# Two-block transformer on one core: attention heads laid into neighbouring weight chunks, and three small moves

## What is computed

```python
for l in range(DEPTH):                       # DEPTH = 2, N_A = 1
    if l == N_A:                             # keys, values, forget gate, once
        kvf = rmsnorm(x, kv_norm) @ w_kvf
        f_logit = (kvf[..., 2 * FOX_WIDTH:] + b_f)
        c_sh = jnp.cumsum(jax.nn.log_sigmoid(f_logit), axis=1)
    x = x + 0.5 * swiglu(rmsnorm(x, ffn_norm[l, 0]), ...)
    h = rmsnorm(x, mix_norm[l])
    mk, mv = split(mem_n @ mem_w_kv[l])      # 4 memory heads of 128
    if l < N_A:
        gate_b, gate_c, u, qm = split(h @ a_w_in)
        y_tok = gate_b * causal_depthwise_conv(gate_c * u, a_conv_w)
        y_mem = memory_attention(qm, mk, mv)
        x = x + concat([y_tok, y_mem]) @ a_w_out
    else:
        q, qm = split(h @ b_w_q)             # 8 heads of 128, 4 memory heads
        y_tok = forgetting_attention(q, k_sh, v_sh, c_sh)
        y_mem = memory_attention(qm, mk, mv)
        x = x + concat([y_tok, y_mem]) @ b_w_out
    x = x + 0.5 * swiglu(rmsnorm(x, ffn_norm[l, 1]), ...)
```

## Time and profile before

| | |
|---|---|
| median of 3 runs | 1873.25 us (1873.0 to 1874.36) |
| the profiled execution: its time, its span | 1875.29 us, 1873.5 us |
| TensorE busy | 1819.4 us, 97% of the span, 9737 matmuls |
| VectorE, ScalarE, GpSimd busy | 65%, 50%, 16% |
| granted TensorE clock, mean | 0.993 of full |
| read from HBM | 318.24 MB, 170 GB/s |

### The profile page before, as it was taken

The page is one execution under the profiler, slowest core; times in us unless marked ns, Lnnn a source line. Parts: engine busy times, 40 slices in busy tenths (PEclk is TensorE's granted clock), DMA queues, the critical chain, the costliest instruction groups (busy, mean ns, idle before and its releaser), DMA issues.

```text
span 1873.5 us, 27530 instructions
## 1 busy us (share of the span) xinstructions
PE 1819.4 (97%) x9737; PEld 1539.3 (82%) x9737; DVE 1211.2 (65%) x1523; ACT 936.3 (50%) x1394; POOL 299.1 (16%) x255
## 2 busy tenths in 40 slices
PE   8899999999999999999999989999999999999998
PEld 6678888888877888888888878888888888778886
DVE  5866755767775665576746756674667656656664
ACT  4455545434456544464545445554554455555553
POOL 1011021211201001210022930002005021020012
PEclk9999999999999999999999999999999999999999
DMA  6326555555521665555555535555555555345553
GB/s 218 130 74 197 180 201 180 180 180 180 180 91 53 195 191 185 195 180 187 193 184 182 186 123 180 193 187 190 182 191 174 185 189 174 108 146 180 188 193 134
DMA packets 215000, 320.29 MB, mean 171 GB/s; under 512 B 6024, under 2 KB 167056, under 8 KB 214672
## 3 DMA queue, kind: packets, MB, share of 16 engines
q1 hardware_dynamic: 213616, 313.45, 50.3%
q0 software_dynamic: 1024, 5.64, 0.8%
q10 hardware_dynamic: 288, 0.23, 0.0%
HBM read 318.24 MB, written 1.06 MB: 170 GB/s over the span
## 4 chain that ended last, share of the span: by engine, by line
PE 91%; DVE 4%; ACT 3%; issue 1%; DMA 1%; DVEq 0%; POOL 0%; POOLq 0%; ACTq 0%; SPq 0%
PE PS L656 26%; PE PS L661 13%; PE PS L663 13%; PE PS L662 13%; PE PS L654 13%; PE PS L650 4%; PE PS L651 2%; PE PS L768 2%; DVE W_lo L1275 2%; PE PS L803 1%; PE PS L786 1%; PE PS L730 1%; ACT U L1096 1%; ACT U L1086 1%; PE PS L919 1%
## 5 line engine op out<-in xcount | busy, mean ns | idle before, releaser
L1275 DVE TENSOR_TENSOR W_lo<-W_raw,W_hi 128x1024 fp32r<-128x1024 f32 x598 | 775.5, 1336 | 292.7 <-ACT W_hi L1012 270.8
L656 PE MATMUL PS<-XN,W_hi 128*128 128x512 f32 x2072 | 740.1, 396 | 0.0
L1012 ACT ACTIVATE W_hi<-W_raw 128x1024 fp32r<-128x1024 f32 x598 | 598.6, 1050 | 176.4 <-PE PS L663 114.5
L654 PE MATMUL PS<-XN,W_lo 128*128 128x256 f32 x2072 | 579.2, 280 | 2.7 <-DVE W_lo L1275 2.7
L656 PEld LDWEIGHTS PS<-XN,W_hi 128*128 128x128 f32 x2072 | 389.6, 188 | 80.2
L654 PEld LDWEIGHTS PS<-XN,W_lo 128*128 128x128 f32 x2072 | 391.4, 189 | 16.6 <-DVE W_lo L1275 3.0
L1809 POOL TENSOR_TENSOR SX<-U,SX 128x512 fp32r<-128x512 f32 (+1 forms) x98 | 128.5, 1315 | 1141.5 <-ACT SX L1079 1141.5
L661 PE MATMUL PS<-W_hi,SX 128*128 128x512 f32 x780 | 303.9, 390 | 1.1 <-DVE W_lo L1275 1.1
L662 PE MATMUL PS<-W_lo,SX 128*128 128x512 f32 x780 | 303.0, 389 | 0.0
L663 PE MATMUL PS<-W_hi,SX 128*128 128x512 f32 x780 | 303.0, 389 | 0.0
L1025 ACT ACTIVATE T<-PS 128x512 f32<-128x512 f32 x152 | 91.0, 599 | 410.5 <-PE PS L656 410.3
(11 more groups left out here) (166 smaller groups left out, 1532.1 us busy)
## 6 DMA issues: line engine op xcount, KB each, us to landing
W_raw<-in_ffn_w_gate_up SPq DMA_DIRECT2D x88, 1024.0 KB, 5.0
W_raw<-in_mlp_w SPq DMA_DIRECT2D x64, 1024.0 KB, 5.2
W_raw<-in_ffn_w_down SPq DMA_DIRECT2D x44, 1024.0 KB, 4.8
W_raw<-in_od_w_in SPq DMA_DIRECT2D x36, 1024.0 KB, 5.1
W_raw<-in_a_w_in SPq DMA_DIRECT2D x14, 1024.0 KB, 4.9
W_raw<-in_mem_w_kv SPq DMA_DIRECT2D x8, 1024.0 KB, 5.1
W_raw<-in_w_kvf SPq DMA_DIRECT2D x8, 1024.0 KB, 5.4
W_raw<-in_ev_w_in SPq DMA_DIRECT2D x6, 1024.0 KB, 6.3
```

Of the source, the lines that this page charges most:

```text
L654: mm(bank[:, S:], wT(W_lo, slot, k, fb), xn[:, k, 0, :], start=False, stop=False)
L656: last = mm(bank, wT(W_hi, slot, k, fb), both, start=False, stop=k == KD - 1)
L1012: A(W_hi[:, slot, halves(h)], W_raw[:, slot, halves(h)], ACT.Copy).then_inc(w_hi, 1)
L1275: V.tensor_tensor(W_lo[:, slot, halves(h)], W_raw[:, slot, halves(h)], W_hi[:, slot, halves(h)], ALU.subtract).then_inc(w_lo, 1)
```

## The change

In `make_plan` the order of the stages changes and the attention stages are marked as woven: a head's steps now stand inside chunks of the neighbouring stages. `steps` says which step stands in which chunk. Step s does `values` of head s-3, `transposes` of head s-2 and `scores` of head s on TensorE; `output` of s-3, `normalise` of s-1 and `soft` of s on VectorE; `keep_pt` of s-2 and `exps` of s on ScalarE. `mem_q` goes ahead of `conv` and of `fox_q`, and `b_out` takes the rows of the memory heads first. Three small moves come with it: at the start the second load waits for the first, the tables wait for the fourth load instead of the second, and two of five dummies go while three new ones stand behind the turn of x; in the gated MLP the logarithm stands one pair of chunks later.

In the diff, the pieces are in this order: the plan, the loads on SyncE, an up and a down chunk on TensorE, a woven step on TensorE, the dummies and the turn of the gate's sums on TensorE, the staging and the gated MLP on ScalarE, a woven step on VectorE, the tables on GpSimd.

```diff
         if l == 0:
-            p.add("conv", "conv", 12, 12, w=w["a_w_in"])
             up("mem_q", w["a_w_in"], 3072, 2, post="copy", dest="mem_q0")
-            p.add("attend", "memory0", what=[("mem0", h) for h in range(4)])
+            p.add("conv", "conv", 12, 12, w=w["a_w_in"], steps={c: [c] for c in range(7)})
+            p.add("attend", "memory0", what=[("mem0", h) for h in range(4)], woven=True)
             down("a_out", w["a_w_out"], 1536)
         else:
-            up("fox_q", w["b_w_q"], 0, 4, post="copy", dest="fox_q")
             up("mem_q", w["b_w_q"], 1024, 2, post="copy", dest="mem_q1")
-            p.add("attend", "fox",
-                  what=[e for h in range(4) for e in (("fox", 2 * h), ("fox", 2 * h + 1), ("mem1", h))])
-            down("b_out", w["b_w_out"], 1536)
+            up("fox_q", w["b_w_q"], 0, 4, post="copy", dest="fox_q",
+               steps={c: [2 * c, 2 * c + 1] for c in range(4)})
+            p.add("attend", "fox", what=[("mem1", h) for h in range(4)] + [("fox", h) for h in range(8)],
+                  woven=True)
+            down("b_out", w["b_w_out"], 1536, order=[4, 5, 0, 1, 2, 3],
+                 steps={0: [8, 9], 1: [10, 11], 2: [12, 13], 3: [14]})
...
             def load(g, slot, src, ks, n):
                 if not isinstance(g, int) or g >= 2:
                     sp.wait_ge(w_lo, 2 * (g - 1))
+                elif g == 1:
+                    sp.wait_ge(raw_full[0], 16)
...
                  for fb, k in sorted(steps, key=lambda x: x[1]) if by_k else steps:
...
+                    if k == 3 and fb < len(woven):
+                        woven[fb]()
...
                 for t in range(TT):
-                    if first and t == 1 and st["src"] == "h" and not st["each"]:
+                    if first and st.get("weave"):
+                        if t == 0:
+                            pe.wait_ge(acc_read, st["u"])
+                    elif first and t == 1 and st["src"] == "h" and not st["each"]:
                         pe.wait_ge(h_done, st["h0"])
...
+                        if at == 2 and t < len(woven):
+                            woven[t]()
...
+            def woven_step(st, s):
+                if s == 0:
+                    pe.wait_ge(r_kept, st["n_rows"])
+                out, turned, scored = (woven_head(st, s - back) for back in (3, 2, 0))
+                if out is not None:
+                    values(heads[out]["unit"])
+                if turned is not None:
+                    transposes(turned)
+                if scored is not None:
+                    pe.wait_ge(acc_read, heads[scored]["q_use"])
+                    scores(heads[scored]["unit"])
...
-            for _ in range(5):
-                mm(PS[:, 0, :], T[:, 0:P], T[:, 0:512], start=True, stop=True)
+            idle_work(3)
...
                         turn(st)
+                        if g0 == 0:
+                            idle_work(3)
...
-                            if st.get("sums") and starts(i, s - 1):
+                            if s == 1 and sums_in(st, i):
                                 between, at = turn_sums, (1, 0)
...
+                elif st["name"] == "a_out" and j < 4:
+                    act.wait_ge(conv_done, j + 1)
+                elif st["name"] == "b_out":
+                    act.wait_ge(h_done, st["h0"] - before_heads(st) + 2 * j + 2)
...
                             if not (st["led"] and starts(i, s)):
                                 ahead(g0 + 2 * i + s, slots[s])
+                            if s == 0 and sums_in(st, i):
+                                act.wait_ge(f_v, 1)
+                                A(f_abs, f_abs, ACT.Exp, scale=-1.0).then_inc(f_a, 1)
+                                act.wait_ge(f_a, 2)
+                                A(f_abs, f_abs, ACT.Ln, bias=1.0).then_inc(f_a, 1)
+                                A(ST[:, 60:61], G[:, 0:1], ACT.Silu)
...
                             cross(g0 + 2 * i + s, u0 + 2 * i + s, pairs[s])
...
+            def woven_step(st, s):
+                out, scaled, scored = (woven_head(st, s - back) for back in (3, 1, 0))
+                if out is not None:
+                    output(heads[out]["unit"])
+                if scaled is not None:
+                    normalise(scaled)
+                if scored is not None:
+                    soft(scored)
...
-            pool.wait_ge(raw_full[1], 16)
+            pool.wait_ge(raw_full[1], 32)
             pool.dma_start(region(R["na_bias"], NA_H * SLOTS * GRID), a["na_bias"]).then_inc(bias_in, 16)
```

More of the change, by code:

```diff
@@ L500, in build_program @@
                 n_staged += st["n"]
-                before = stages[n - 1]
+                before = stages[n - 2 if stages[n - 1].get("woven") else n - 1]
                 before["next_down"] = st
                 st["each"] = before["kind"] == "glu" or before.get("dest") == "h"
-            if st["kind"] == "attend":
+                st["bank"] = [4, 6]
+            if st["kind"] == "attend" and not st["woven"]:
                 stages[n - 1]["next_attend"] = st
-        before_heads = lambda st: len(stages[stages.index(st) - 1]["what"])
+            if st["kind"] == "attend" and st["woven"]:
+                for near in (stages[n - 1], stages[n + 1]):
+                    if near.get("steps"):
+                        near["weave"] = st
+                if stages[n + 1].get("steps"):
+                    pair = stages[n + 1]["u"] % 2
+                    stages[n + 1]["low_banks"] = [2 * pair, 2 - 2 * pair]
+        before_heads = lambda st: len(stages[stages.index(st) - 1]["what"])
+        for n, st in enumerate(stages):
+            if st.get("low_banks"):
+                st["bank"] = st["low_banks"]
+            if st["kind"] == "norm":
+                st["down_bank"] = stages[n - 1].get("bank", [4])[0] if n else 4
+            if st["kind"] == "attend" and st["woven"]:
+                use = {q["name"]: q["u"] for q in stages[:n] if q["name"] in ("mem_q", "fox_q")}
+                for what, h in st["what"]:
+                    e = next(e for e in heads if e["st"] is st and (e["bias"] == "fox", e["h"]) == (what == "fox", h))
+                    e["q_use"] = use["fox_q" if what == "fox" else "mem_q"] + h // 2 + 1
         def e_out_done(n):
@@ L512, in e_out_done, with woven_head, row_block @@
                     return st["h0"] + n - st["a0"] + 1
+        def woven_head(st, s):
+            at = st["weave"]
+            return at["a0"] + s if 0 <= s < len(at["what"]) else None
+        def row_block(st, j):
+            return st["order"][j] if st.get("order") else j
         def raw_count(g, slot):
@@ L534, in build_program, with after_first, sums_in @@
         starts = lambda i, s=0: isinstance(i, int) and i == 0 and s == 0
-        def after_first(engine, n, body):
-            body(0)
-            repeat(engine, n - 1, lambda i: body(i + 1))
+        def after_first(engine, n, body, first=1):
+            for i in range(first):
+                body(i)
+            repeat(engine, n - first, lambda i: body(i + first))
+        def sums_in(st, i):
+            return bool(st.get("sums")) and isinstance(i, int) and i == 1
         block = ctx.enter_context(nc.Block())
@@ L888, in body @@
                                      first=s == 0 and (starts(i) or not st["raised"]),
-                                     between=between, at=at, by_k=st["led"] and starts(i, s))
+                                     between=between, at=at, by_k=st["led"] and starts(i, s),
+                                     woven=woven_steps(st, 2 * i + s) if "weave" in st else ())
                     if n > 1:
-                        after_first(pe, n // 2, body)
+                        after_first(pe, n // 2, body, 2 if st.get("sums") else 1)
                     if n % 2:
@@ L981, in _ @@
                         turn_heads(R["mla_kn"], 2 * pairs[b] - 2 * b, range(4 * b, 4 * b + 4))
-                elif kind == "attend":
-                    a0, m = st["a0"], len(st["what"])
+                elif kind == "attend" and not st["woven"]:
                     pe.wait_ge(acc_read, u0)
                     us = st["units"]
-                    if not st["paired"]:
-                        for u in us[opened(st):3]:
-                            scores(u)
                     for u in us:
@@ L997, in _ @@
                             scores(u + 2)
-                        if not st["paired"] and u + 3 in us:
-                            scores(u + 3)
                         values(u)
@@ L1166, in _ @@
                     else:
-                        repeat(act, loops, body)
-                    if early:
+                        repeat(act, loops, body, straight="weave" in st)
+                    if early and st["name"] != "fox_q":
                         stage_early(early)
@@ L1240, in _ @@
                     stage_early(st["next_down"])
-                elif kind == "attend":
-                    a0, m = st["a0"], len(st["what"])
```

(4 more changed lines are left out.)

145 lines of the change are left out of this document (85 added, 60 removed).

## The result

The changed kernel took 1877.87 us (median of 8 runs, 1874.61 to 1879.13), the kernel before 1873.12 us (8 runs, 1871.45 to 1874.78): a ratio of 1.0022, 95% interval 1.0013 to 1.0031. Forecast were 1873.5 us, within 1866.5 to 1880.5, with "same" likelier (0.52) than "slower" (0.27). The time lies in the range. The change is slower by 0.22% (0.13 to 0.31), just over the 0.2% that was put as the bound of what can be told; by the medians it is 4.75 us. And 1877.87 lies 0.9 us above the narrower range, 1870 to 1877, that stood for the forecast's own sum.

A forecast was written before the change was run, and what follows sets the result against it. TensorE was taken to bound the dense stage, so changes count only through its waits and low clock. Terms +11.6 - 7.5 - 1.6 - 2.4 = +0.1 us gave 1873.5 us, range 1866.5 to 1880.5.

The forecast's parts named there:

- Place 1: memory0, conv into a_out: stall 17.1, low clock 2.5, woven waits 0.3, less 8.3 removed: +11.6 us.
- The stall: Ahead of a_out: TensorE stands still until GpSimd's last conv chain and first low part are done, 17.1 us.
- The chain: GpSimd's operations for the last conv column block, then a_out's first low part: 14.5 us, starting 2.6 us after the last chunk.
- The clock: Behind the gap ahead of a_out: TensorE at the lower clock, 1.7 to 3.5 us lost, taken as 2.5.
- Place 2: fox, heads woven into fox_q and b_out: 12.4 us of losses removed; gap 2.4, clock 1.2, waits 1.3 added: -7.5 us.
- the rival in which VectorE's queue paces the woven chunks: Woven attention chunks: heads keep their earlier waits, fox_q chunks take over 9.8 us; 5 us more, 1878.5 us; 18%.
- Place 3: The gate in the gated MLP: 4.5 us of losses removed, waits of 1.4 and 1.5 added: -1.6 us.
- The second wait: At the gate: VectorE's split held by GpSimd's later bias tables, put at 1.5 of 0 to 4 us.
- Place 4: The start: earlier first matmul and third load, but norm factor behind the tables: -2.4 us, between -4.5 and +1.
- two rivals (1878.5 and 1879): VectorE's queue pacing woven chunks, 1878.5 us, 18%; a longer a_out stall, longer low clock and bad start, 1879 us, 12%.
- the seam is dearer: Into a_out: stall 19.0 us and low clock for 7 us, +2.9, plus the start's bad end, +3: 1879 us; 12%.

The follow-up runs named there:

- the filled stall: Changed kernel plus 80 dummy matmuls on TensorE between the last conv chunk and a_out: 1873.61 us, ratio 0.9996 to the kernel before.
- the first experiment: Changed kernel with GpSimd making a_out's first two low parts ahead of the last conv column block's chain: 1870.78 us, ratio 0.9980 to the kernel before.
- the kernel with the tables spread: Changed kernel with the gate's bias tables made piece by piece behind low parts of ffn_down on GpSimd: 1879.01 us, ratio 1.0030 to the kernel before.

## Why the prediction was right, and where it was not

**Place 1** was forecast at +11.6 us and measured at +12.2. The stall: 17.1 forecast, 17.65 measured. The chain from its first operation to the end of the first low part took 14.4 us where the prediction summed 14.5, which also decides between its two bounds for the stall (17.1 if the chain is faster without VectorE beside it, 19.0 if GpSimd is simply that slow). It began 3.2 us after the last chunk, not 2.6, since `by_rows` took 1.61 us, not 0.69, beside GpSimd's product of the block before. The clock: 2.5 forecast, 6.1 us at half measured, 3.1 lost; the filled stall shows that the standing still was its cause. With VectorE's split beside it the same pair of scalings took 3.88 us instead of 1.82 (in the first experiment, at 1100.62). The waits in the woven chunks, put at 0.3, did not occur here; three other executions have one, of 0.83, 0.43 and 0.34 us, for `normalise` in a woven `conv` chunk at 1047.

**Place 2** was forecast at -7.5 and measured at -7.7: a gap of 2.30 us (2.4), 1.7 us of clock (1.2, between 0 and 1.7), 0.3 us of waits in the woven chunks (1.3). The wait of `values` came in the third chunk of `b_out`, where the prediction had it, with 0.3 instead of 1 us. A `fox_q` chunk with its heads took 8.5 us (34.05 by four), where over 9.8 would have spoken for the rival in which VectorE's queue paces the woven chunks. So that rival is wrong: a head whose partners had a chunk's time waits for almost nothing. That -7.7 comes so close to -7.5 is in part luck: the waits were put 1.0 us too high and the clock 0.5 too low.

**Place 3** failed in size: -1.6 forecast, +0.6 measured. The two waits were 1.04 and 1.93 us, together 2.97 where 2.9 was put. What the sum lacks is the step behind them: 3.4 us at the low clock after the second gap, 1.7 lost, and half a microsecond at its edges. The prediction gives the clock a term at both seams and none here, and states no reason; the gap of 2.73 us before had no fall behind it. A gap of this size is followed by a fall in some executions and not in others (below), so each such gap should have had half a term. The second wait, put at 1.5 of 0 to 4 us, rests on a guess of the phase: that it came at 1.93 is luck.

**Place 4** was right in its mechanism: the first matmul of weights at 11.05 (11.2), the factor ready at 25.6 (25.9), the chunk at 30.66 (30.9). The forecast of -2.4 agrees with what was left in the pair of profiles at the next stage, 2.17 us, where TensorE waited for a split, longer than before. Timelines of TensorE, before and changed:

```profile
46.89 0.47 PE L661 MATMUL PS<-W_hi,SX 128*128 128x512 f32 x1 [1.09 <-DVE W_lo L1275]
44.72 0.47 PE L703 MATMUL PS<-W_hi,SX 128*128 128x512 f32 x1 [1.70 <-DVE W_lo L1373]
```

It agrees too with the 2 us over all profiled executions. In this pair 1.2 of it is left at the second turn of x, since the low clock at the end of the first attention lasted 6.82 us in the changed kernel, and in the kernel before half as long:

```profile
112.26:115.67 3.41, 2.98 (x14) 1.82 (x10) 0.43 (x1) 1.41 (x3) 2.50 (x2) 0.50 0.00 0
```

So the forecast of +0.1 missed the +3.9 of the last turn by 3.8, 2.2 of it at place 3, 1.2 at place 4, 0.6 at place 1, with place 2 the other way by 0.2. By its number the result is nearer to two rivals (1878.5 and 1879) than to the sum, and neither took place: the woven chunks hardly waited, and the chain took 14.4 us, not the 16.4 that a stall of 19.0 needs; of "the seam is dearer" only the longer low clock came, worth 0.6 us. That no change was forecast and a small one measured is thus a matter of place 3's missing term and of one late draw at the start. "The saving at the attention is paid back by the conv chain" is what happened, and the payback was for the most part avoidable (16.6 of 20.7 us): with the order of GpSimd's queue mended, the same weave, the repairs at the gate and `b_out` and the norm's factor ahead of the tables are together worth 1.3%.

## What to carry to other kernels

When work that stood between two stages is moved away, look at what it was covering on the other engines, and above all at queues in which the next stage's first operation stands behind the last stage's longest chain: lay that operation into the chain where it is due, and compute for each one when it is due. Count a possible fall of the clock behind every gap of two to three microseconds, with half its price, and its full price behind one of about four or more (all 21 here). GpSimd, whose long subtractions held VectorE here, should get many short instructions beside VectorE's work, not a few long ones.

## What the runs showed of the hardware

The low clock behind a gap is not settled by the length of the gap. Behind the same gap of 1.93 us at the gate, six profiled executions have 3.4 us at the low level and one has none; behind the same gap of 2.30 us at `b_out` six have it and three have none; behind 2.50 and 2.73 us there was none, behind 2.91 and 17.65 there was. Over all twelve traces (one of each kernel), 26 of the 44 gaps of 1.9 to 3.0 us are followed by a stretch at the lower level, and all 14 gaps between 3.7 and 4.5 us. In four of the twelve even two gaps of 0.96 and 0.81 us, one behind the other at about 585, have some 3 us of it behind them. A fall costs some 1.7 us behind most of the gaps of two to three, and 3.4 behind those of 2.91 and 2.96 us. That these falls make much of the scatter between runs of one kernel is not shown by traces, as each kernel has one, but the runs point to it: of 28 runs of the kernel before, the longer ones have the lower mean clock (0.991 to 0.995, correlation with the time -0.78). The Trainium skill (TensorE: Matmul & The Clock Gate, section on the HAM clock gate) says that the monitor which sets the clock runs free of the kernel; these rows agree with that, and cannot prove it.

VectorE and GpSimd hold each other up in both directions. VectorE's 0.69 us operation on two tiles of SBUF (L1622) took 3.78 beside the subtractions at the gate, the largest of which took 4.49 in the kernel with the tables spread, and GpSimd's 0.61 us addition with one input took 2.62 beside a split. VectorE's operation just ahead of it (L1389, 1424.10), which reads PSUM and one tile of SBUF, took its usual 0.69 us in the midst of the same subtractions. That is the exclusion that the prediction cites from the Trainium skill (SBUF — State Buffer, section "two separate sides"), for a small GpSimd operation too; the one VectorE instruction with a single SBUF input stands outside it, as by that page it should.
